# Gate and up projections of an FFN by seven block products in place of eight

## The reference, cut to what matters

```python
def rmsnorm(x, g):
    y = xf * lax.rsqrt(jnp.mean(xf * xf, axis=-1, keepdims=True) + EPS)
    return (y * g.astype(jnp.float32)).astype(x.dtype)
...
    h = h + (mg[:, :, 0] * a + mg[:, :, 1] * s) @ lw['w_o']
    f = rmsnorm(h, lw['ffn_norm'])
    h = h + (jax.nn.silu(f @ lw['w_ffn_gate']) * (f @ lw['w_ffn_up'])) @ lw['w_ffn_down']
    g = jax.nn.sigmoid(rmsnorm(h, lw['ple_norm']) @ lw['w_ple_gate'])
    return h + g * (p_l @ lw['w_ple'])
```

## Time and profile before

| | us |
|---|---|
| median of 3 runs (lowest, highest) | 1114.2 (1109.92, 1116.05) |
| the profiled execution's own time | 1115.03 |
| its span in the profile | 1113.2 |
| PE busy (share of the span) | 1066.8 (96%) |
| DVE, ACT, POOL busy | 471.7, 405.5, 345.9 |
| granted TensorE clock, mean | 0.983 of 2.4 GHz |

### The profile page before, as it was taken

The page is one execution under the profiler, slowest core; times in us unless marked ns, Lnnn a source line. Parts: engine busy times, 40 slices in busy tenths (PEclk is TensorE's granted clock), DMA queues, the critical chain, the costliest instruction groups (busy, mean ns, idle before and its releaser), DMA issues.

```text
span 1113.2 us, 20077 instructions
## 1 busy us (share of the span) xinstructions
PE 1066.8 (96%) x8625; PEld 1015.8 (91%) x8625; DVE 471.7 (42%) x975; ACT 405.5 (36%) x702; POOL 345.9 (31%) x169
## 2 busy tenths in 40 slices
PE   5999999999999999988999999999999999999996
PEld 4899999998999966656899999999999999999995
DVE  4996886104432247753673243322322320110544
ACT  5456322344222267855323332222223222222313
POOL 2542322331000010021435524334334444544320
PEclk9899999998999999999999999999999999999998
DMA  9543273867238015156623322332323322332402
GB/s 234 125 107 97 77 231 89 255 189 238 87 72 103 1 44 221 49 167 215 195 79 93 89 83 80 92 94 78 95 80 92 90 78 81 93 93 82 132 20 81
DMA packets 164707, 125.23 MB, mean 112 GB/s; under 512 B 21195, under 2 KB 153771, under 8 KB 162828
## 3 DMA queue, kind: packets, MB, share of 16 engines
q1 hardware_dynamic: 160696, 106.92, 35.0%
q0 software_dynamic: 3456, 16.78, 4.4%
q10 hardware_dynamic: 468, 0.27, 0.1%
HBM read 110.18 MB, written 15.69 MB: 113 GB/s over the span
## 4 chain that ended last, share of the span: by engine, by line
PE 84%; DVE 4%; ACT 3%; issue 3%; POOL 2%; DMA 2%; SPq 1%; ACTq 1%; DVEq 0%; POOLq 0%
PE pair L1810 20%; PE pair L1812 20%; PE pair L1811 19%; PE pair L1992 3%; PE pair L1993 3%; PE pair L1994 3%; PE pair L1817 3%; PE pair L2138 2%; POOL ring_r L743 2%; PE pair L2115 1%; PE pair L2125 1%; DMA ring<-in_w_in 1%; PE pair L1987 1%; DVE arena L1240 1%; SPq L611 1%
## 5 line engine op out<-in xcount | busy, mean ns | idle before, releaser
L743 POOL TENSOR_TENSOR ring_r<-ring,ring_r 128x1024 fp32r<-128x1024 f32 (+2 forms) x123 | 293.5, 2395 | 491.5 <-ACT ring_r L852 489.0
L1811 PE MATMUL pair<-uT_r,ring_r 128*128 128x272 f32 (+1 forms) x1328 | 383.9, 289 | 0.0
L1810 PE MATMUL pair<-arena_r,ring_r 128*128 128x272 f32 (+1 forms) x1008 | 297.0, 295 | 5.4 <-DVE uT_r L1240 3.3
L1812 PE MATMUL pair<-arena_r,ring_r 128*128 128x272 f32 (+1 forms) x1008 | 294.0, 292 | 0.0
L1810 PE MATMUL pair<-zT_r,ring_r 128*128 128x272 f32 x928 | 270.5, 292 | 0.0
L1812 PE MATMUL pair<-zT_r,ring_r 128*128 128x272 f32 x928 | 268.5, 289 | 0.0
L1811 PEld LDWEIGHTS pair<-uT_r,ring_r 128*128 128x128 f32 (+1 forms) x1328 | 250.8, 189 | 0.7
L1810 PEld LDWEIGHTS pair<-arena_r,ring_r 128*128 128x128 f32 (+1 forms) x1008 | 190.8, 189 | 7.8 <-DVE uT_r L1240 4.2
L1812 PEld LDWEIGHTS pair<-arena_r,ring_r 128*128 128x128 f32 (+1 forms) x1008 | 190.7, 189 | 0.4
L1810 PEld LDWEIGHTS pair<-zT_r,ring_r 128*128 128x128 f32 x928 | 174.7, 188 | 0.4
L1812 PEld LDWEIGHTS pair<-zT_r,ring_r 128*128 128x128 f32 x928 | 174.6, 188 | 0.0
(11 more groups left out here) (332 smaller groups left out, 1377.8 us busy)
## 6 DMA issues: line engine op xcount, KB each, us to landing
ring<-in_w_in SPq DMA_DIRECT2D x26, 512.0 KB, 4.2
ring<-in_w_ffn_gate SPq DMA_DIRECT2D x22, 512.0 KB, 3.8
ring<-in_w_ffn_up SPq DMA_DIRECT2D x22, 512.0 KB, 3.8
ring<-in_w_ffn_down SPq DMA_DIRECT2D x16, 512.0 KB, 4.0
gate_spill<-arena SPq DMA_DIRECT2D x16, 272.0 KB, 5.1
ring<-in_w_o SPq DMA_DIRECT2D x8, 512.0 KB, 4.0
ring<-in_w_ple_gate SPq DMA_DIRECT2D x8, 512.0 KB, 4.0
arena<-gate_spill SPq DMA_DIRECT2D x2, 1904.0 KB, 13.2
```

What stands on the lines that cost most here:

```text
L743: eng.tensor_tensor(ring_r[:, n % RING, 0:slab_size(n)], ring[:, n % RING, 0:slab_size(n)], hi, ALU.subtract).then_inc(S["slab_split"], 1)
L1810: eng.matmul(out, w_hi, x_hi(k)[:, cols], start=n == 0, stop=False)
L1811: eng.matmul(out, w_hi, x_lo(k)[:, cols], start=False, stop=False)
L1812: ins = eng.matmul(out, w_lo, x_hi(k)[:, cols], start=False, stop=n == len(steps) - 1)
```

## The change

Gate and up of one chunk are taken together as a 2x2 block product: the two rows are the gate's and the up's 128 columns, the contraction is halved (pieces 0 to 3 and 4 to 7), and so are the tokens (272 each). Eight block products of 12 matmuls (4 pieces x 3 terms) become seven (the scheme of Strassen, in Winograd's form), numbered 1 to 7 in `product(i, c)`.

- **Tokens' sums** X1 to X4 (`t_parts`, `t_low`): made once by DVE while w_o runs, with high parts by ACT.
- **Weights' sums** S1 to S4 (`weight_sum`): four DVE subtractions or additions of 128x512 for each chunk. Of the parts A11, S1, S2, A12, S3, A22, S4 ACT writes the high parts (`half_high`) and DVE the low parts (`half_low`); POOL has no part in gate and up any more.
- **Weights in SBUF:** gate and up of a chunk land in one set of 4096 columns that also holds S1 to S4; two sets in the old ring take turns, a third in the arena serves chunk 0.
- **Results.** Products 1, 6, 7 and 4 add up in one bank, 5 and 3 in another, 2 in a third. Between them ACT copies the running sum out (`keep`), and DVE forms the four results (`c11`, `c22`, `c12`, `middle`).
- **The norm's factor** goes on the gate alone (in `c12`) and on down's result, where DVE now multiplies by `rs` before it adds to the residual.
- **mid's high and low parts** are all made in the last chunk and after it, since the places of the high parts hold the tokens' sums until then. Down's first weights are loaded and split there too.

```diff
+def products():
+    out = [(1, 0)]
+    for c in range(FC):
+        out += [(5, c), (6, c), (2, c), (7, c)] + [(1, c + 1)] * (c + 1 < FC) + [(4, c), (3, c)]
...
+            for c in range(3, FC):
+                eng.wait_ge(*product_done(2, c - 2))
+                load_gate(c)
+                eng.wait_ge(*product_done(4, c - 2))
+                load_up(c)
+            eng.wait_ge(*product_done(2, FC - 2))
+            load_slab(FIRST_DOWN)
...
             for c in range(FC):
...
+                s, more = c % 2, c + 1 < FC
+                if c and more:
+                    half_high(c + 1, "A11")
                 if c:
...
+                    silu(c - 1)
+                keep(c, 1, 6, bank_a[s])
+                if more:
+                    for part in ("S1", "S2", "A12", "S3"):
+                        half_high(c + 1, part)
+                else:
+                    for m in range(4):
+                        mid_part(m)
+                keep(c, 2, 7, bank_a[s])
+                if more:
+                    half_high(c + 1, "A22")
+                    half_high(c + 1, "S4")
+                    keep(c + 1, 0, 1, bank_a[1 - s])
+                else:
+                    for m in range(4, 12):
+                        mid_part(m)
...
+            eng.wait_ge(*product_done(3, FC - 2))
+            weights_high(first)
+            silu(FC - 1)
+            for m in range(12, 16):
+                mid_part(m)
...
+            def t_parts(k):
+                n1, n2 = slice(0, HT), slice(HT, TT)
+                eng.tensor_scalar(uT[:, k, :], hT[:, k, :], vec[:, 8 + k:9 + k], None, ALU.mult).then_inc(S["u_new"], 1)
+                eng.wait_ge(S["u_new"], KC + k + 1)
+                if k < 4:
+                    tt(X1[:, k, :], uT[:, k, n2], uT[:, k, n1], ALU.subtract).then_inc(S["t_new"], 1)
+                    return
+                j, made = k - 4, 4 + 3 * (k - 4)
+                tt(X3[:, j, :], uT[:, k, n2], uT[:, j, n2], ALU.subtract).then_inc(S["t_new"], 1)
+                tt(X2[:, j, :], uT[:, k, n2], X1[:, j, :], ALU.subtract).then_inc(S["t_new"], 1)
...
+                tt(uT_r[:, j, n2], X1[:, j, :], f32(u_hi[:, j, n2]), ALU.subtract).then_inc(S["t_split"], 1)
...
+                tt(X4[:, j, :], uT[:, k, n1], X2[:, j, :], ALU.subtract).then_inc(S["t_new"], 1)
...
+            def c12(c):
+                eng.wait_ge(*product_done(3, c))
+                tt(sil[:, c % 2, HT:TT], bank(bank_c[c % 2])[:, 0:HT], kept[1], ALU.add).then_inc(S["c_made"], 1)
+                eng.wait_ge(*past("c_made", 3 * c + 3))
+                tt(sil[:, c % 2, :], sil[:, c % 2, :], rs, ALU.mult).then_inc(S["gate_scaled"], 1)
+
+            def middle(c):
+                eng.wait_ge(S["silu_done"], c + 1)
+                eng.wait_ge(*product_done(4, c))
+                tt(mid[:, c, 0:HT], bank(bank_a[c % 2])[:, 0:HT], sil[:, c % 2, 0:HT], ALU.mult)
+                tt(mid[:, c, HT:TT], mid[:, c, HT:TT], sil[:, c % 2, HT:TT], ALU.mult).then_inc(S["mid_new"], 1)
...
             for c in range(FC):
...
+                more = c + 1 < FC
+                if c == 1:
+                    eng.wait_ge(*past("root_done", 1))
+                    link(eng.reciprocal(rs, rt))
                 if c:
...
+                    c12(c - 1)
+                    if more:
+                        half_low(c + 1, "A11")
+                    middle(c - 1)
+                    if more:
+                        for q in range(1, 4):
+                            weight_sum(c + 1, q)
+                c11(c)
+                if more:
+                    weight_sum(c + 1, 4)
+                    half_low(c + 1, "S1")
+                    half_low(c + 1, "S2")
+                else:
+                    for m in range(4):
+                        mid_low(m)
+                c22(c)
+                if more:
+                    for part in ("A12", "S3", "A22", "S4"):
+                        half_low(c + 1, part)
...
-                eng.tensor_tensor(halves(hT[:, c, :]), halves(hT[:, c, :]), both(pair_of[("down", c)]), ALU.add).then_inc(taken[pair_of[("down", c)]], 1)
...
+                eng.tensor_tensor(halves(rt), both(pair_of[("down", c)]), halves(rs), ALU.mult).then_inc(taken[pair_of[("down", c)]], 1)
                 eng.wait_ge(*out_of(("down", c)))
+                link(tt(hT[:, c, :], hT[:, c, :], rt, ALU.add))
...
+            def product(i, c):
...
+                if i == 6:
+                    eng.wait_ge(*past("part_kept", 3 * c + 1))
+                if i == 7:
+                    eng.wait_ge(*past("part_kept", 3 * c + 2))
+                if i == 4:
+                    eng.wait_ge(*past("part_kept", 3 * c + 3))
+                if i == 3:
+                    eng.wait_ge(*past("c_made", 3 * c + 2))
+                eng.wait_ge(*past("half_split", half_count(c, PART_OF[i])))
...
+                for k in range(4):
+                    x_hi, x_lo = moving[i](k)
+                    ins = three_terms(out, hi[:, k * P:(k + 1) * P], lo[:, k * P:(k + 1) * P], x_hi, x_lo, fresh and k == 0, k == 3, not fresh)
+                ins.then_inc(S["product_done"], 1)
```

More of the change, by code:

```diff
@@ L151, in plan_gemms @@
         group(("wo", c), plain_steps(slab("wo", c), KC))
-    for c in range(FC):
-        for kind in ("gate", "up"):
-            group((kind, c), plain_steps(slab(kind, c), KC))
-            if (kind, c) == ("gate", 0):
-                group(("norm", 1), None)
     for m in range(KC):
@@ L1203, in down_parts @@
+            first = split_index[step_slab("wo", KC - 1)] + 1
+            eng.wait_ge(*product_done(3, FC - 2))
[3 more added lines that the diff above has]
+                mid_part(m)
+            weights_high(first + 1)
+            for m in range(16, FC):
+                mid_part(m)
+            weights_high(first + 2)
             def down_parts(k):
@@ new lines, in _ @@
+            for n, (i, c) in enumerate(product_list):
+                product(i, c)
+                if (i, c) == (4, 0):
+                    eng.wait_ge(S["sq_added"], KC - 1)
+                    eng.wait_ge(*out_of(("wo", KC - 1)))
+                    for h in range(2):
+                        ins = eng.matmul(bank(norm_banks[h])[:, 0:HT], ones, sq_sum[:, h * HT:(h + 1) * HT], start=True, stop=True)
+                    ins.then_inc(S["norm_sum"], 1)
+            eng.wait_ge(S["mid_new"], FC - 1)
```

257 lines of the change are left out of this document (217 added, 40 removed).

## The result

| | before | after |
|---|---|---|
| median of 4 runs (lowest, highest), us | 1113.59 (1109.92, 1116.05) | 1094.48 (1093.13, 1095.12) |
| ratio, 95% interval | | 0.9835, 0.981 to 0.9859 |
| the profiled execution, us (its span) | 1115.03 (1113.2) | 1095.12 (1093.3) |

The change makes the kernel 1.65% faster, 19 us, and the interval leaves out no change; forecast were 18.5 less and 1096.

The account below looks back on a forecast made before the run. PE's number of matmuls was taken as the bound in gate and up: 233.0 + 8.9 (head) + 7.3 (tail) = 249.2 us for 268.5, 0.8 back behind down, so 18.5 less than 1115.0: 1096, range 1089 to 1104.

Parts of the forecast that it names:

- What is removed: Gate and up: 84 matmuls a chunk in place of 96, 10.59 us for 12.10, so 33.3 us go over 22 chunks.
- DVE in the middle: Middle chunks of gate and up: DVE needs 9.6 us, PE 10.59, so PE stays the bound with 1 us to spare.
- The rule: DVE's next operation waits until the pipe is empty; the prediction held that it starts earlier, 0.65 us for 0.72.
- The rival built on this: Every DVE operation costs its full duration: 10.8 us a chunk, over PE's 10.59, time 1100 to 1101; chance 0.12.
- the slow one: Waits make DVE the bound in gate and up: some 12.4 us a chunk, time 1135; chance 0.09.
- The head: From w_o's last matmul through chunk 1: PE waits and the low clock cost 8.9 us, norm included; bounds 5.9 and 12.
- they wait for DVE anyway; I add 0.9: Start of gate and up: products slowed by the low clock wait for DVE anyway, so the clock adds only 0.9 us.
- The tail: Last chunk and down's start: product 4 0.5 us late, PE idle 4.85, clock 2; 7.3 us in all, bounds 4.5 and 9.
- The clock's 2 us: Low clock behind PE's idle time ahead of down: 2 us lost, between none and twice that.
- Behind down: DVE multiplies by `rs` before adding; only the last chunk's is on the path, 0.8 us more.
- POOL's last square, sets the norm: Behind down, the path of the last chunk was said to end in POOL's last square and PE's norm.
- The sum: Gate and up 233.0 + 8.9 + 7.3 = 249.2 us for 268.5; 0.8 back, 18.5 less in all, time 1096.

## Why the prediction was right, point by point

- **What is removed.** 10.59 us a chunk was forecast, 10.55 measured. The 33 us are there in full; 14 of them are given back ahead of down's first matmul.
- **DVE in the middle.** 9.6 us with 1 us to spare: measured 9.58 (10.55 - 0.97), and the two added operations put the free time at 1.09. The waits inside a chunk cost PE nothing, as counted.
- **The rule.** The low parts start 0.605 apart and last 0.68. The Trainium skill, VectorE: DVE Perf Modes, section The DRAIN you can't avoid, taken without its last sentence (the next operation starts when the pipe is empty), would have made DVE the bound; the trace sides with its addition, that an operation which is not held starts earlier. The rival built on this falls with the idle 0.97, and so does the slow one: chunks of 12.4 us would need 1.8 more, and DVE reached 11.23 only with 1.77 us of extra work.
- **The head.** Forecast 8.9 us, and this is the mis-sized term. DVE came 2.3 late (2.5), PE's first wait was 3.27 (3.7), and product 6 began 8.56 after product 1 (8.5). But product 4 of chunk 1 began at 30.56, where 27.6 and 0.9 for the clock were forecast: 2.1 more. The step that failed is "they wait for DVE anyway; I add 0.9". It holds for products 5 and 6: the wait ahead of product 6 shrank from 1.8 to 0.53 because product 5 ran slowly. It doesn't hold for products 2 and 7, nor for product 1 of the next chunk, since the clock stayed low for 10 us, and not for the 3 to 4 read from the earlier trace rows. With the clock held up the head was 1.95 shorter: that is the clock's price. The other 1.0 are small waits: chunk 1's product 7 starts at 24.7 there (24.3), product 4 at 28.56 (27.6).
- **The tail.** 0.5 and 4.85 us of waiting were forecast, 0.49 and 4.90 came, by the operations named: eight mid parts on ACT (4.48 us), then the slab's high part, then POOL's low part, as the rows above show. The clock's 2 us are right in size (4.4 us at half speed lose 2.2), but holding the clock up gave back only 0.9: with PE faster a third split of POOL fell into DVE's row of low parts, and PE waited 0.86 for them.
- **Behind down.** 0.8 us: the multiplication is there, 0.75 on DVE. From DVE's first row behind the last chunk to the norm it is 7.42 before and 7.58 after, so 0.2 of it arrived at the end. The step that failed is that POOL's last square, sets the norm: it ended at 1039.64 before, and PE was at its own matmuls without a gap until the norm at 1040.37. POOL's row after is this:

```profile
1019.23 1.36 POOL L897 TENSOR_TENSOR arena<-arena 128x544 f32<-128x544 f32 x1
```

The square now ends 7.44 behind DVE's first row, for 6.69: the 0.75 are all there. PE's own matmuls hid some 0.6 of them, and now the norm does wait for the square.
- **The sum.** Gate and up with the clock's 2 us: 249.2 forecast, so 247.2 without them; measured 248.91. The head's 2.1 us too few, and what was too many in the middle (0.04 x 22 = 0.9), are the difference but for 0.5. The tail's two waits cost 0.4 of that, since a bracket counts from the end of the row before: from start to start PE lost 5.05 us at 877.69 (872.51 to 877.69, less 0.13) and 0.64 at 869.51, where a slower first matmul took another 0.1, 5.8 for the 5.39 in the brackets. Gate, up and down together gave 17.2 us in place of 18.5; the time of the profiled run came out 1.4 us under the forecast all the same, since the stretch ahead of gate was 2.5 shorter. That the forecast lies so near is in part luck.

## What to carry to other kernels

When work goes from PE to an engine that is hidden, count that engine's whole loop from start to start, and prove the room by adding an operation: one was free here, two were not. The ends, where the pipeline fills and drains, cost as much attention as the middle: 14 of 33 us went there, and 10 came back by the order of a few instructions on ACT and DVE, by one split moved from POOL to DVE, and by matmuls that keep PE busy. When a wait is removed, look at once for what is late next; here a slab two steps on took half of the gain until it too was moved. And look at how long the late operation took, not only at when it began: the split was late because it stood still.
